# One projection chunk between the two bursts of small products of each inversion level of a gated delta rule, three behind them in place of four

## The reference, cut to what matters

```python
lower = jnp.where(strict, jnp.einsum("bhnid,bhnjd->bhnij", kb, k) * decay, 0.0)
rhs = jnp.concatenate([vb, kb * jnp.exp(g)[..., None]], axis=-1)
sol = lax.linalg.triangular_solve(lower, rhs, left_side=True, lower=True, unit_diagonal=True)
```

## Time and profile before

| what | value |
|---|---|
| median of 3 runs | 1191.27 us (1190.1 to 1191.54) |
| the profiled execution's own time | 1189.98 us |
| its span | 1188.3 us |
| TensorE busy | 1169.5 us, 98% of the span |
| VectorE busy | 914.9 us, 77% |
| ScalarE busy | 606.6 us, 51% |
| GpSimd busy | 59.5 us, 5% |
| granted TensorE clock | 9 or more tenths of full speed in all 40 slices |

### The profile page before, as it was taken

The page is one execution under the profiler, slowest core; times in us unless marked ns, Lnnn a source line. Parts: engine busy times, 40 slices in busy tenths (PEclk is TensorE's granted clock), DMA queues, the critical chain, the costliest instruction groups (busy, mean ns, idle before and its releaser), DMA issues.

```text
span 1188.3 us, 21262 instructions
## 1 busy us (share of the span) xinstructions
PE 1169.5 (98%) x7959; PEld 1005.2 (85%) x7959; DVE 914.9 (77%) x1428; ACT 606.6 (51%) x952; POOL 59.5 (5%) x98
## 2 busy tenths in 40 slices
PE   7999999999999999999999999999999999999998
PEld 4689999888888887777787878888889999998887
DVE  5779999798886793788586567579799999988552
ACT  5536666332222575766773435444546666654331
POOL 1000000001110000000402110003000000000000
PEclk9999999999999999999999999999999999999999
DMA  9653333798773233222233222864233333342440
GB/s 325 191 161 107 105 106 106 229 289 272 239 232 104 71 106 90 54 54 71 54 90 108 63 75 80 248 193 143 72 106 107 106 106 106 106 135 74 112 115 27
DMA packets 235063, 152.63 MB, mean 128 GB/s; under 512 B 8021, under 2 KB 216046, under 8 KB 234990
## 3 DMA queue, kind: packets, MB, share of 16 engines
q1 hardware_dynamic: 230890, 149.62, 43.2%
q10 hardware_dynamic: 4100, 2.02, 0.6%
HBM read 145.31 MB, written 6.29 MB: 128 GB/s over the span
## 4 chain that ended last, share of the span: by engine, by line
PE 88%; DVE 5%; ACT 3%; DMA 1%; issue 1%; SPq 0%; ACTq 0%; DVEq 0%
PE tail L2359 8%; PE tail L2363 7%; PE tail L2368 7%; PE region L2450 7%; PE region L2454 7%; PE region L2447 7%; PE tail L2349 5%; PE tail L2351 5%; PE tail L2350 5%; PE region L2359 3%; PE region L2363 3%; PE region L2368 3%; PE tail L2447 2%; PE tail L2454 2%; PE tail L2450 2%; PE region L2349 2%
## 5 line engine op out<-in xcount | busy, mean ns | idle before, releaser
L872 ACT ACTIVATE w_hi<-raw 128x1024 fp32r<-128x1024 f32 (+1 forms) x147 | 165.1, 1123 | 246.3 <-PE tail L2368 142.4
L1445 DVE TENSOR_TENSOR w_lo<-raw,w_hi 128x1024 fp32r<-128x1024 f32 (+1 forms) x144 | 188.5, 1309 | 59.4 <-ACT w_hi L872 59.1
L2349 PE MATMUL tail<-u_hi,w_hi 128*128 128x512 f32 x264 | 107.7, 408 | 0.9 <-DVE w_lo L1445 0.9
L2351 PE MATMUL tail<-u_hi,w_lo 128*128 128x512 f32 x264 | 103.1, 391 | 0.0
L2350 PE MATMUL tail<-u_lo,w_hi 128*128 128x512 f32 x264 | 103.0, 390 | 0.0
L1653 DVE TENSOR_TENSOR w_lo<-raw,w_hi 128x512 fp32r<-128x512 f32 (+1 forms) x124 | 86.8, 700 | 14.4 <-ACT w_hi L944 10.0
L1455 DVE SCALAR_TENSOR_TENSOR ada_acc<-ada_raw,cond,ada_acc 128x512 f32<-128x512 f32 x98 | 73.5, 750 | 3.9
L944 ACT ACTIVATE w_hi<-raw 128x512 fp32r<-128x512 f32 x92 | 58.0, 631 | 15.5 <-DVE raw L1670 9.6
L948 ACT ACTIVATE work<-region 128x256 f32<-128x256 f32 x106 | 40.1, 378 | 49.1 <-PE region L2454 29.0
L2359 PE MATMUL tail<-g_hi,w_hi 128*128 128x512 f32 x264 | 64.3, 391 | 0.0
L2363 PE MATMUL tail<-g_lo,w_hi 128*128 128x512 f32 x264 | 64.1, 390 | 0.0
(11 more groups left out here) (525 smaller groups left out, 2702.1 us busy)
## 6 DMA issues: line engine op xcount, KB each, us to landing
raw<-in_w_ffn_in SPq DMA_DIRECT2D x168, 256.0 KB, 3.2
ada_raw<-in_w_ada SPq DMA_DIRECT2D x56, 512.0 KB, 5.1
raw<-in_w_in SPq DMA_DIRECT2D x90, 256.0 KB, 3.3
raw<-in_w_ffn_out SPq DMA_DIRECT2D x32, 384.0 KB, 4.5
raw<-in_w_ffn_out SPq DMA_DIRECT2D x32, 320.0 KB, 3.7
ada_early<-in_w_ada SPq DMA_DIRECT2D x8, 1024.0 KB, 10.8
gates<-kept_gates SPq DMA_DIRECT2D x16, 256.0 KB, 3.0
raw<-in_w_out SPq DMA_DIRECT2D x16, 256.0 KB, 3.3
```

The source lines that it names most:

```text
L872: act.activation(w_hi[:, slot % 2, 0:k, :], raw[:, slot, 0:k, :], ACT.Copy).then_inc(hi_ready, 1)
L1445: dve.tensor_tensor(w_lo[:, slot % 2, 0:k, :], raw[:, slot, 0:k, :], w_hi[:, slot % 2, 0:k, :].bitcast(f32), ALU.subtract).then_inc(lo_rea ...
L2349: pe.matmul(bank(b), wh, xh, start=start and n == 0, stop=False)
L2351: ins = pe.matmul(bank(b), wl, xh, start=False, stop=stop and n == k - 1)
```

## The change

Inside the loop over levels 1 to 4, one chunk is issued between the first burst (both blocks) and the second burst (both blocks), and three instead of four behind the second. The call behind the join at L2887 keeps its 4 chunks. The number of chunks in front of every later point is the same as before, and the lists of ScalarE, VectorE, GpSimd and SyncE are untouched.

```diff
@@ -2853,6 +2853,7 @@
                                 ins = pe.matmul(region[e][part(r), h * QB:(h + 1) * QB], link[part(r), e, h, 0:QB],
                                                 inv[part(r), e, h, 0:QB], start=True, stop=True)
                         ins.then_inc(prod_ps, 1)
+                    fill("level", 1)
                     for b in both:
                         e = b % 2
                         pe.wait_ge(prod_ready, 2 * JOIN * pair + 2 * (l - 1) + e + 1)
@@ -2863,7 +2864,7 @@
                                 ins = pe.matmul(region[e][part(r), S + h * QB:S + (h + 1) * QB], inv[part(r), e, h, HB:HB + QB],
                                                 prod[part(r), e, h, 0:QB], start=True, stop=True)
                         ins.then_inc(corr_ps, 1)
-                    fill("level")
+                    fill("level", FILL["level"] - 1)
                 for b in both:
                     e = b % 2
                     pe.wait_ge(inv_ready, 2 * JOIN * pair + 2 * (JOIN - 2) + e + 1)
```

## The result

The changed kernel takes 1194.46 us (median of 8 runs, 1192.59 to 1195.77), the kernel before 1191.09 us (8 runs, 1190.02 to 1192.21). The ratio is 1.0027, with a 95% interval of 1.0018 to 1.0035: slower by 3.2 us, between 2.1 and 4.2 (the two medians lie 3.4 apart). Run again beside 27 runs of the kernel before it was 1193.66 against 1190.37, a ratio of 1.0029 (1.0020 to 1.0038). The forecast was 1193.1 us, +1.8.

The account below looks back on a forecast made before the run. TensorE, busy 98% of the span, was taken as the bound. 6 x 0.03 + 0.44 + 1.15 = +1.8 us on the median 1191.27 gave 1193.1 us, range 1190.0 to 1195.2.

Parts of the forecast that it names:

- the levels: Sign of being wrong: levels 2 and 3 lasting over 4.6 or under 4.4 us.
- the stretches: First burst of level 1 to first chunk behind the join, each pair; sign of being wrong unless near 20.9 and 20.5 us.
- Part 1: Chunk between bursts, levels without another wait: ScalarE wait goes, switches cost about as much; +0.03 us per level, +0.2 for eight.
- Part 2: Level 1 of pair 0: the moved chunk must wait for the low part of its weights from VectorE; +0.44 us.
- Part 3: Level 4 and join: VectorE's transposes start later with less cover, the join's last burst waits; +1.15 us for both pairs.
- the hitch: Level 4, pair 1: first burst took 0.93, not 0.75 us; if repeated, level with join takes 7.00, not 6.86.
- the second sentence of the text: In the two stretches before the change: TensorE busy 19.09 and 19.29 of 19.81 and 19.86 us, clock full.
- The first: Rival at the second bursts: ScalarE wait goes and little takes its place; in full -1.8 us, 1189.5; chance 0.14.
- The second: Rival at each level's two new switches: 128-wide to 32-wide changes drain the array; +1.5 us for eight, 1194.6; chance 0.18.
- The third: Rival behind the changed levels: a later TensorE wait swallows the shift; about 1191.3 us; chance 0.08.
- Hidden work: Later VectorE work stays within slack; tightest is level 3 of pair 1, where 0.4 us remains.

Follow-up runs that it names:

- switches_only: Against the changed kernel: moved chunk kept only at levels 2 and 3 of pair 0 and levels 1 to 3 of pair 1; 1190.60 us, ratio 1.0001.
- change_again: The changed kernel run once more without an edit, beside the kernel before; 1193.66 us, ratio 1.0029.
- cover_level4: Against the changed kernel: four chunks stay behind level 4 and three instead of four come behind the join; 1191.60 us, ratio 1.0008.
- only4_covered: Against the kernel before: chunk between the bursts at level 4 only, four chunks still behind it, three behind the join; 1191.16 us, ratio 1.0002.
- less_cover: Against the kernel before: no chunk between bursts, three chunks behind level 4 and five behind the join; 1192.99 us, ratio 1.0022.
- only_level4: Against the changed kernel: moved chunk kept at level 4 only; 1195.07 us, ratio 1.0038, and run again 1193.54 us, ratio 1.0030.
- not_level4: Against the changed kernel: moved chunk kept at levels 1 to 3 only, level 4 as before; 1191.10 us, ratio 1.0007.
- more_cover_again: Second run of the kernel before with five chunks behind level 4 and three behind the join, none between bursts; 1189.96 us, ratio 0.9994.
- cover_both: Kernel before with five chunks behind level 4, three behind the join, three in front of the solve, four behind it; 1189.21 us, ratio 0.9987.
- two_between: Against the changed kernel: two chunks between the bursts at all levels and two behind them; 1197.33 us, ratio 1.0057.

## Why the prediction was right or wrong

**The range held, the size did not.** 1194.46 is inside 1190.0 to 1195.2, but the loss of 3.2 us is nearly twice the forecast 1.8, and it lies past the 2.4 us of 0.2% that the text took as the bound (the interval begins at 2.1): the outcome was "slower", to which the text gave 0.27, and not "no change that can be told", to which it gave 0.68. Of the text's own signs of being wrong the levels held; the stretches came out at 21.10 and 20.80 in place of 20.9 and 20.5. That the range holds the result owes something to its upper end, which was set by a rival that did not come true.

**Part 1 held.** The sum had a level of 4.51 to 4.52 and a second burst at 1.57; measured 4.53 (633.48 to 638.01), 4.55, 4.52, 4.54 and 4.55, and 1.58. What takes the wait's place, the switches, was priced from the join's single chunk, and that row was right to 0.03 us a level. switches_only shows it alone: +0.1 us.

**Part 2 held but for 0.1.** Level 1 of pair 0 took 5.04 in place of 4.48, +0.56, where 0.44 + 0.03 was forecast. The difference is the semaphore behind VectorE: 0.05 in the text, taken from ScalarE's copy, 0.15 measured (629.52 to 629.67).

**Part 3 held as a mechanism and was small by 0.1 in pair 0 and 0.2 in pair 1.** The join's burst waits for VectorE's last transpose, as said. The chain measured 0.53 + 4.35 as said; the semaphore behind it was again 0.15 and not 0.05 (649.02 to 649.17). Level 4 with the join took 6.98, forecast 6.87, and 7.19 in pair 1, forecast 6.86 or 7.00: the hitch in the first burst came again (0.95 in the changed kernel, 1.12 in change_again, 0.93 before); what causes it no run shows. cover_level4, only4_covered and less_cover show from three sides that the cover of this chain is the cause, not the chunk between the bursts.

**The step that failed is the second sentence of the text**, "its clock full (1.00, the 2.4 GHz level)", taken from the kernel before and used for the kernel after without being asked again. Of the 1.4 us between the forecast and the loss, 0.5 lies in the two stretches (2.23 where 1.75 was forecast: the semaphore, 0.1 in three places, and the hitch of pair 1) and about 1 outside them. For that 1 us the sum has no term: the forecast priced TensorE's wait at the join at its own length and nothing more. Where TensorE stood still for 0.75 us in the midst of the small bursts, the granted clock fell behind it in part of the executions, and each fall cost 1.6. That, 1.6 behind one join in one of the two profiles of the change and behind both in both profiles of only_level4, is what I take to lift a loss of 2.2 to 2.4 to a median of 3.2: the three executions of the first run at a mean clock of 1.000 took 1193.05 on average, 2.0 above the median of before, the five others 1194.9. The step from the falls to the median is argued: only one execution of each run has a trace. In the sum of the text it would have been one more term of part 3, with a bound above of 3.2.

**The rivals.** The first (the wait goes, little takes its place) is out by switches_only: five of its waits gone, and nothing won. The second, the slower one, had the right sign for the wrong reason: the Trainium skill's rule that a change of tiling mode drains the engine (TensorEngine Tiling (Array Packing), section Key Properties) is not contradicted, but the whole visit of a chunk costs 0.24 more than its stream time, which is also what the row had, and not 0.43. The estimate by the Trainium skill (TensorE: Matmul & The Clock Gate, section Single matmul latency), 0.33 a level, was too high: by it a level would take 4.61, and the levels without another wait took 4.52 to 4.55. The third is out: nothing was won back, and from the end of the second stretch to the end of the span both kernels take 482.5 us.

**Hidden work stayed hidden.** Level 3 of pair 1 was named as the tightest place; VectorE reported its second block at 704.06 (703.81 + 0.25) and level 4's burst began at 704.27, without a wait.

## What to carry to other kernels

A chunk of filler has two jobs, to fill a gap and to cover a chain; before moving one into a gap, look at what it covers where it stands, above all at the last step of a loop, whose successor may wait for more than the steps in between did. Price the switch into and out of the filler from a place where the trace already has it: a gap of 0.22 us was here not worth filling. And where the change makes the busiest engine stand still longer than it did, add the clock as a term of its own; the same chunks moved the other way (one more in front of the join, one more in front of the solve) gave the only gain.

## What was not expected of the hardware

- The granted clock fell to the 1.2 GHz level behind waits of 0.75 us of TensorE, in bursts of 32x32 matmuls in which it was recorded as busy for 1.43 of 2.43 us (647.11 to 649.54, first burst of the join to the first chunk; 1.46 of 1.79 from 644.58 to 646.37 in the kernel before). In profiles without such a wait (not_level4, cover_level4, only4_covered, more_cover_again, cover_both) it stayed at 1.00 there. But the wait does not settle it: change_again (busy for 1.45 of 2.44) and two_between have waits as long or longer and no fall in their profiles. The Trainium skill (TensorE: Matmul & The Clock Gate, section Part 1: The HAM clock gate) puts such a fall down to an engine that was not busy; the trace agrees in that every fall behind a join followed a wait. What decides it from one execution to the next stays open. One thing goes with it in these few profiles: the three with falls (the change, both of only_level4) also had a mean clock of 0.97 in their first 60 us, and the two with the same wait and no fall (change_again, two_between) had 1.00 there. A start at 0.97 is not enough by itself: less_cover, with waits of 0.41 and 0.57, and cover_level4 had it too, and no fall behind a join.
- When it fell, seven or eight distances in a row between the large matmuls behind the join were 0.40 to 0.43 us in place of 0.23, from the first matmul on in the change and up to four matmuls later in only_level4; in the next burst the clock was full again. The cost, 1.6, was the same in all five falls of three profiles (the change and both of only_level4): 4.54 or 4.55 us from the first chunk matmul behind the join to the next burst, which takes 2.94 at full clock.
- TensorE went on 0.14 or 0.15 us after a VectorE result for which it waited (629.52 to 629.67, 649.02 to 649.17) and 0.05 after ScalarE's copy out of PSUM (636.41 to 636.46 in the kernel before), but 0.14 after ScalarE's scaled keys (715.60 to 715.74, kernel before). The forecast had taken the 0.05 for all.
